# Down-projection by seven products: two of four weight sums made by adding transfers, products one and five moved into the turn ahead, a fifth turn in the second column group

## What is computed

```python
u = causal_dwconv(jnp.einsum('bsd,df->bsf', h2, w_up[l]), conv_w[l], conv_b[l])
u_gate, u_val = u[..., :D_FF], u[..., D_FF:]
x = x + jnp.einsum('bsf,fd->bsd', jax.nn.silu(u_gate) * u_val, w_down[l])   # f: 256 x 5632, w_down: 5632 x 2048
```

## Time and profile before

| what | value |
|---|---|
| median of 3 runs | 2069.29 us (2069.28 to 2069.82) |
| profiled execution, its own time | 2069.8 us |
| its span, first to last instruction | 2067.9 us |
| mean granted TensorE clock | 1.000 |
| PE busy | 2062.2 us (100%) |
| DVE busy | 1671.4 us (81%) |
| ACT busy | 1179.0 us (57%) |
| mean DMA rate | 206 GB/s |

### The profile page before, as it was taken

How to read it: one execution, slowest core, us unless ns; L and a number is a source line. 1 busy time by engine, 2 the same in 40 slices (tenths; PEclk the granted TensorE clock), 3 DMA queues, 4 the chain that set the end, 5 groups by cost and what they waited for, 6 DMA issues and landing times.

```text
span 2067.9 us, 25525 instructions
## 1 busy us (share of the span) xinstructions
PE 2062.2 (100%) x9884; PEld 1730.1 (84%) x9884; DVE 1671.4 (81%) x1880; ACT 1179.0 (57%) x1405; POOL 55.3 (3%) x59
## 2 busy tenths in 40 slices
PE   9999999999999999999999999999999999999999
PEld 8888888888888887888888888888888888888887
DVE  7988888887897887887788778867777777789986
ACT  6766555555556566666555555555555555555553
POOL 0000000000000010110000000000000000000000
PEclk9999999999999999999999999999999999999999
DMA  9667777787784677755575656455555555556663
GB/s 341 213 199 219 225 234 225 212 241 220 249 266 154 208 226 236 219 176 186 150 233 179 207 183 217 161 183 183 184 192 191 188 199 180 192 185 234 227 206 126
DMA packets 118584, 426.44 MB, mean 206 GB/s; under 512 B 13248, under 2 KB 14016, under 8 KB 118208
## 3 DMA queue, kind: packets, MB, share of 16 engines
q1 hardware_dynamic: 109440, 394.66, 56.8%
q0 software_dynamic: 6048, 22.02, 6.1%
q10 hardware_dynamic: 2976, 8.14, 1.2%
HBM read 422.67 MB, written 2.10 MB: 205 GB/s over the span
## 4 chain that ended last, share of the span: by engine, by line
PE 95%; DVE 2%; DMA 1%; ACT 1%; issue 1%; ACTq 0%; DVEq 0%
PE g L973 47%; PE xs L1019 10%; PE xs L826 8%; PE g L826 8%; PE g L1023 7%; PE g L797 4%; PE xs L832 4%; PE g L832 4%; DVE w_lo L1897 1%; PE xs L875 1%; DMA raw<-in_stream 1%; PE xs L1060 1%; PE xs L1196 0%; ACT w_hi L1401 0%; PE xs L1193 0%
## 5 line engine op out<-in xcount | busy, mean ns | idle before, releaser
L1897 DVE TENSOR_TENSOR w_lo<-raw,w_hi 128x1024 fp32r<-128x1024 f32 x621 | 752.3, 1221 | 274.1 <-ACT w_hi L1401 266.9
L1401 ACT ACTIVATE w_hi<-raw 128x1024 fp32r<-128x1024 f32 x621 | 651.1, 1057 | 500.7 <-PE g L973 204.3
L973 PE MATMUL g<-w_hi,in_both 128*128 128x512 f32 x1104 | 350.4, 390 | 0.0
L973 PE MATMUL g<-w_hi,mid_both 128*128 128x512 f32 x864 | 280.4, 393 | 0.0
L973 PEld LDWEIGHTS g<-w_hi,in_both 128*128 128x128 f32 x1104 | 207.2, 188 | 43.0
L973 PE MATMUL g<-w_lo,in_both 128*128 128x512 f32 x552 | 214.7, 389 | 0.0
L973 PEld LDWEIGHTS g<-w_hi,mid_both 128*128 128x128 f32 x864 | 162.2, 188 | 33.5
L973 PE MATMUL g<-w_lo,mid_both 128*128 128x512 f32 x432 | 168.2, 389 | 0.0
L826 PE MATMUL g<-mlp_both,w_hi 128*128 128x512 f32 x704 | 167.0, 391 | 0.0
L826 PE MATMUL xs<-mlp_both,w_hi 128*128 128x512 f32 x704 | 165.6, 390 | 0.0
L826 PEld LDWEIGHTS xs<-mlp_both,w_hi 128*128 128x128 f32 x704 | 130.7, 188 | 26.2
(11 more groups left out here) (532 smaller groups left out, 3524.7 us busy)
## 6 DMA issues: line engine op xcount, KB each, us to landing
raw<-in_stream SPq DMA_DIRECT2D x621, 512.0 KB, 4.2
d_block<-in_stream SPq DMA_DIRECT2D x28, 512.0 KB, 4.7
o_block<-in_stream SPq DMA_DIRECT2D x24, 512.0 KB, 4.8
v_block<-in_stream SPq DMA_DIRECT2D x20, 512.0 KB, 4.4
gm_block<-in_stream SPq DMA_DIRECT2D x16, 512.0 KB, 5.5
ge_block<-in_stream POOLq DMA_DIRECT2D x15, 512.0 KB, 5.5
ge_block<-in_stream SPq DMA_DIRECT2D x10, 512.0 KB, 5.0
gl_block<-in_stream POOLq DMA_DIRECT2D x6, 512.0 KB, 5.4
```

Of the source, the lines that this page charges most:

```text
L973: ins = mm(GG[:, bank, :], a[:, kt, t * P:(t + 1) * P], w[:, slot, half_chunk(j)], start=n == 0 and opens(item, bank), stop=ended and n == ...
L1401: activation(w_hi[:, n % RING, :], of[:], ACT.Copy).then_inc(hi_ready, 1)
L1897: v.tensor_tensor(w_lo[:, n % RING, :], of, w_hi[:, n % RING, :].bitcast(F32), ALU.subtract).then_inc(lo_ready, 1)
```

## The change

In the down-projection, and there alone:

- The order is a new table, `DOWN_STEPS`, of (plain turn, turn whose products 7, 6, 3, 2, 4 are done here, turn whose products 1 and 5 are done here). Products 1 and 5 of a turn move into the step ahead of its other five. A full step is in the order `BOTH_QUADS`: C0 3 7 C1 6 2 4 1 C2 5 C3; a group's first such step is `FIRST_QUAD`, its last `LAST_QUAD` (C0 3 7 C1 6 2 4 C2 C3).
- Group 1 does a fifth turn by products (turn 10), with its sums of f made at item 76 and two more places for them. Group 0 ends with plain turn 10 mixed with the last products of turn 2, group 1 with plain turn 9 mixed with those of turn 10.
- Two of the four weight sums (for products 7 and 6) are made by transfers that POOL issues and that add B22 into B12 and into B11. DVE makes the other two, that for 4 out of the ring's `raw` block of product 2. The blocks of products 3 and 2 come through the ring.
- The blocks B11 and B12 have two sets, used turn about, loaded two turns ahead.

```diff
-    "down": (((3, None), (4, None), (8, None), (9, None), (5, 0), (6, 1), (7, 2), (10, None)),
-             ((3, 0), (7, None), (4, 1), (5, 2), (8, 6), (9, None), (10, None))),
...
+DOWN_STEPS = (((3, None, None), (4, None, None), (8, None, None), (9, None, None),
+               (5, None, 0), (6, 0, 1), (7, 1, 2), (10, 2, None)),
+              ((3, None, 0), (4, 0, 1), (5, 1, 2), (7, 2, 6), (8, 6, 10), (9, 10, None)))
...
-SUMS_AT = {"v": (4, 8), "out1": (2, 6), "vv": (-7, 3), "down": (3, 7, 11, 64), "gm0": (-8, -5), "out2": (-7,)}
+SUMS_AT = {"v": (4, 8), "out1": (2, 6), "vv": (-7, 3), "down": (3, 7, 11, 64, 76), "gm0": (-8, -5), "out2": (-7,)}
...
-SPREAD = ("ug", "vv", "side")
+SPREAD = ("ug", "vv", "side", "down")
+TWO_SUMS = ("vv", "side", "down")
...
+LATER, FIRST = (7, 6, 3, 2, 4), (1, 5)
+BOTH_QUADS = ("C0", 3, 7, "C1", 6, 2, 4, 1, "C2", 5, "C3")
+FIRST_QUAD = ("C0", "C1", 1, "C2", 5, "C3")
+LAST_QUAD = ("C0", 3, 7, "C1", 6, 2, 4, "C2", "C3")
...
-             FIRST_ITEM["down"] + 13: ("down", B22), FIRST_ITEM["down"] + 14: ("down", B21),
+             FIRST_ITEM["down"] + 13: ("down", B11, 1), FIRST_ITEM["down"] + 14: ("down", B12, 1),
...
-                if next_in_place(item) is not None and quad_of(item) + 1 < len(QUADS):
-                    q = quad_of(item)
-                    if QUADS[q + 1][0] == item.phase:
+                after = 2 if item.phase == "down" else 1
+                if next_in_place(item) is not None and quad_of(item) + after < len(QUADS):
+                    q = quad_of(item) + after
+                    if QUADS[q][0] == item.phase:
                         sp.wait_ge(lo_ready, n + 1)
-                        load_block(q + 1, next_in_place(item))
+                        load_block(q, next_in_place(item))
...
-                elif item.phase in MID_ORDER and item.product == 2:
+                elif item.phase in TWO_SUMS and item.product == 2:
                     dve.wait_ge(lo_ready, n + 1)
                     to = wide(item.phase, item.group).blocks[buffer_of(quad_of(item), B11)]
                     v.tensor_tensor(to[:], to[:], raw[:, CHUNK_COUNT[n] % RING, :], ALU.add).then_inc(sem["block_sums"], 1)
```

More of the change, by code:

```diff
@@ L173 @@
                     ITEMS.append(Item(_name, _g, 0, _turn, _k // 2, 2 * _turn + _k % 2))
+        continue
+    if _name == "down":
+        for _g, _steps in enumerate(DOWN_STEPS):
+            for _turn, _later, _first in _steps:
+                _order = PLAIN if _later is None else LAST_QUAD
+                if _first is not None:
+                    _order = FIRST_QUAD if _later is None else BOTH_QUADS
+                for _what in _order:
+                    if _what in PLAIN:
+                        _k = int(_what[1])
+                        ITEMS.append(Item("down", _g, 0, _turn, _k // 2, 2 * _turn + _k % 2))
+                    else:
+                        ITEMS.append(Item("down", _g, _what, _first if _what in FIRST else _later, None, None))
         continue
@@ L290, in loads_of_block, with beside @@
     return sum(not second(k) and (QUADS[k][0] not in SPREAD or b in (B11, B12)) for k in range(q + 1))
+def beside(q):
+    return q < len(QUADS) and QUADS[q][0] in MID_ORDER and QUADS[q][2] == MID_SECOND
 def second(q):
-    return QUADS[q][0] in MID_ORDER and QUADS[q][2] == MID_SECOND
+    return beside(q) or QUADS[q][0] == "down" and (q - quads_ahead("down")) % 2 == 1
 def spread_quads(q):
@@ L326, in sums_made @@
 def sums_made(q, p):
-    ahead = sum(1 if phase == "ug" else 2 if phase in MID_ORDER else 4 for phase, _, _ in QUADS[:q])
-    if second(q):
+    ahead = sum(1 if phase == "ug" else 2 if phase in TWO_SUMS else 4 for phase, _, _ in QUADS[:q])
+    if beside(q):
         return ahead + {5: 0, 4: 2}[p]
-    if q + 1 < len(QUADS) and second(q + 1):
+    if beside(q + 1):
         return ahead + {5: 1, 4: 3}[p]
-    return ahead + ({5: 1, 4: 2} if QUADS[q][0] in MID_ORDER else {5: 1, 7: 2, 6: 3, 4: 4})[p]
+    return ahead + ({5: 1, 4: 2} if QUADS[q][0] in TWO_SUMS else {5: 1, 7: 2, 6: 3, 4: 4})[p]
 def buffer_of(q, b):
@@ L734, in _ @@
                     sp.wait_ge(lo_ready, n + 1)
-                    if item.phase in MID_ORDER and item.product == 2:
+                    if item.phase in TWO_SUMS and item.product == 2:
                         sp.wait_ge(sem["block_sums"], sums_made(quad_of(item), 4))
@@ L765, in _ @@
                         sp.wait_ge(sem["y_ready"], GROUPS)
-                    load_block(QUADS.index((phase, of[0], of[1] if len(of) > 1 else MID_TURN)) if of else quads_ahead(phase), b)
+                    if of and phase == "down":
+                        load_block(quads_ahead(phase) + of[0], b)
+                    else:
+                        load_block(QUADS.index((phase, of[0], of[1] if len(of) > 1 else MID_TURN)) if of else quads_ahead(phase), b)
                 if n in GAIN_AT:
@@ L1389, in high_of_chunk @@
                         act.wait_ge(*block_in(q, b))
-                    elif item.phase in SPREAD and item.product != 5 and not (item.phase in MID_ORDER and item.product == 4):
+                    elif item.phase in SPREAD and item.product != 5 and not (item.phase in TWO_SUMS and item.product == 4):
                         act.wait_ge(*block_added(q, item.product))
```

8 lines of the change are left out of this document (4 added, 4 removed).

## The result

| what | before | after |
|---|---|---|
| median of 6 runs each, taken side by side | 2069.49 us | 2077.78 us (2076.64 to 2078.24) |
| ratio | | 1.0039, interval 1.0028 to 1.0050 |
| profiled execution, its own time | 2069.8 us | 2077.61 us |
| its span | 2067.9 us | 2075.8 us |

The change makes the kernel slower by 8.3 us, 0.39%. The forecast was 2076.3, its range 2072.3 to 2078.8, so the time lies inside, 1.5 above the point. The two profiled spans differ by 7.8.

What follows compares the result with a forecast made beforehand. PE was taken as the bound, DVE close behind. -1.36 - 0.08 + 2.8 + 2.55 + 1.10 + 2.06 = +7.07, called +7.0, on the runs' median 2069.29 gave 2076.3 us, range 2072.3 to 2078.8.

Steps and rivals of the forecast that it cites:

- part 1: Down-projection on PE: 1008 matmuls instead of 1014, -1.36 us, and the one 0.08 us loss goes too.
- part 2: Full steps: a chain of hops makes C2's low part late, PE waits 0.47 us in each of six, +2.8.
- part 3: Sums of f at item 64 delay C3's low part, +1.10 us; the new set at item 76 costs 0.
- part 4: Change of column group: the add of banks 0 and 1 behind three pairs holds PE's write, +2.55 us.
- part 5: Program's end: DVE's last add ends 2.84 us after PE, not 0.78, +2.06; transfers out 0 to 0.5, taken as 0.
- part 6: POOL's adding transfers for products 7 and 6 and SP's refills land in time: 0 us.
- the count of 9.99: Full step, from PE's end of product 3: C2 is ready after 9.99 us, PE wants it at 9.52.
- That for 6 has more: Adding transfer for product 6 has more room to land than the 9.6 us of that for 7; cost 0.
- third rival: Adding transfers land late, making product 7 late in turns by products: +10.2 us, 2079.5, or +20; chance 0.09.
- The first two rivals: Steps keep up, C2 and C3 not late: 2072.5 us, chance 0.14; change of group hidden too: 2069.9, chance 0.05.
- the sum would have been 8.8: Alternative sum of +8.8 us if each independent DVE start cost 0.08 more, in full steps, change of group and end.

Runs made afterwards that it cites:

- combined kernel with the later loads: Changed kernel, all four places mended, B11 and B12 of turn 1 loaded at items 17 and 18, not 13 and 14: 2069.38 us, 0.9999 of before.

## Why the prediction was right

Term by term, forecast and profile of the changed kernel:

| term | forecast | measured |
|---|---|---|
| part 1, six matmuls | -1.36 | -1.36 |
| part 1, small waits elsewhere | -0.08 | +0.43 |
| part 2, C2 of six full steps, 0.463 each | +2.8 | +2.78 |
| part 3, C3 | +1.10 | +1.09 |
| part 4, change of group | +2.55 | +2.47 |
| part 5, last add behind PE | +2.06 | +2.15 |
| part 5, transfers out | 0 to 0.5, taken as 0 | +0.03 |
| part 6, adding transfers (C2 of the third full step, 0.84) | 0 | +0.38 |
| start of the stretch | | -0.14 |
| sum | +7.07 | +7.83 |

**The places were right**, all four of them, and each was taken away by itself: C2 by the order of product 4, C3 by the sums of f, the change of group by a plain turn, the end by the fifth turn undone. **Part 2's hops** came in another order: the sum for 4 started 1.26 behind 2's low part (1.36 in the forecast), the next turn's sum 1.35 behind that of 1 (1.26). The two errors cancel. The reason given beside them, that two sums stand close together, was the weaker half: with product 4 moved they stand closer, and C2 is in time. The hop over ACT that the count of 9.99 contains is what decides.

**What was mis-sized is part 6**: the sentence "That for 6 has more" held for the other full steps, where landings of 6.3 to 8.5 us cost nothing, but not for the third, the first full step of group 1:

```profile
1960.91 0.86 POOL L2668 DMA_DIRECT2D d_block<-in_stream  x1 [4.10 <-DVE w_lo L1926]
```

```profile
1970.78 1.06 ACT L1430 ACTIVATE w_hi<-d_block 128x1024 fp32r<-128x1024 f32 x1 [2.45 <-DMA d_block<-in_stream]
```

The transfer for 6 was issued 4.97 behind that for 7 (4.08 at the same place of group 0), DVE being late behind the change of group. It landed 9.85 later at 1970.76, and C2 waited 0.84. The one delay met the other; the forecast had priced each place as if the step ahead of it were in time. The wait fell to 0.46 without transfers, and also with the change of group mended by the plain turn. ACT waited nine times for an adding transfer, 13.8 us in all, which the prediction names as a sign of its third rival; little of it reached PE: without the transfers PE's stretch is 235.40, 0.57 shorter, which is this step's 0.38 and small waits.

The **small waits** were forecast to go, and grew: 0.11 at product 4 of the third full step, a place not named, and 65 starts of 0.229 to 0.240 us, mostly behind a wait, where before had 8 (up to 0.282); they add 0.40 (0.09 before). Nor was the 0.08 of part 1 the only loss before: the other wait of the earlier trace rows, 0.08 at 1856 us, stands in both kernels. The median rose by 8.3 and the profiled span by 7.8; runs of the changed kernel scatter over 1.6 us, those of before over 0.7, and this half microsecond isn't settled. Of the 1.5 by which the forecast falls short, the terms of the table account for 0.8.

The first two rivals did not come about: DVE's smaller load did not make the low parts run ahead, and the order held the add of banks 0 and 1 behind the pairs. The third came about in one step of the changed kernel, and in the experiment with the plain turn behind group 0's pairs, there through loads issued close by. That DVE holds POOL up does not show: POOL's issue took 862 to 902 ns in all sixteen cases, beside a DVE that was 80% busy.

By the Trainium skill, VectorE: DVE Perf Modes, section The DRAIN you can't avoid, the sum would have been 8.8, nearer to the median's 8.3 than my 7.1, and farther from the profile's 7.8. The rows do not bear out its sentence that the next operation does not start until the pipe is empty: two low parts in a row took 2.35 us at 1943.42 in the changed kernel, so the second started 1.13 after one of 1.22. They agree with the one behind it in that section, that an operation which is not held starts earlier.

## What to carry to other kernels

An engine that is 80% busy can be late at one place in each step; whether it is, is worked out by counting hops from the place that is freed to the item that is wanted, not from its share. Taking work off such an engine gains nothing if what is left puts one more hop ahead of the item that is wanted: here the same 191 us of DVE cost 7 us of PE's waits in one order and next to none in another. Even so, the kernel with every place mended is not told by its times from the one before the change. When the waits are gone, look at what the transfers do next, at the start (loads beside adding transfers) and at the end (four transfers out at once).

## What was not expected of the hardware

- In the changed kernel, of two adding transfers of 512 KB issued 2.35 us apart the second landed in 7.3 to 9.0 us, the first in 5.5 to 6.9; the first pair of the combined kernel with the later loads, 6.3 us apart and with no load into `d_block` in the 8 us ahead of either, in 5.2 and 5.65. Whether they go one after the other was not tried. By the Trainium skill, DMA: Bandwidth & Descriptors, section Anatomy of one DMA — SWDGE (gpsimd) path, one takes 2.0 us and its bytes over 436 GB/s, by estimate 3.2 here; the shortest of the changed kernel took 5.1, beside other loads.
- Behind a wait of PE of 2.5 us the granted clock fell once, to a mean of 0.60 over 4.3 us, matmuls up to 0.43 apart where 0.227 is the distance at full clock, so at 1.2 of 2.4 GHz for part of it; five other profiles with the same wait kept full clock. It cost 1.6 us.
- Transfers out of 128 KB took 1.8 to 2.2 us where the one of 512 KB had been issued 2.5 us or more ahead of them, and 3.3 to 3.4 where it was 0.9 to 1.3.
